# Forgetting attention: two heads side by side in the array, and later weight pieces

## The chip, the cores and the metric

The kernel runs on one core of a Trainium2 chip. The metric is the device time of one execution in microseconds, the median of the runs.

## What is computed

Two transformer blocks on 1024 rows of width 1024, in float32. The second block mixes three attentions: a latent one (4 heads, values of 128), a forgetting one (4 heads of 64) and a chunked one (4 heads of 64). The change is in the forgetting attention and in the latent one behind it. The forgetting attention, cut to what matters:

```python
def _fox(q, k, v, f_logit, f_bias):            # 4 heads of 64
    log_f = jax.nn.log_sigmoid(f_logit + f_bias)
    cum = jnp.cumsum(log_f, axis=1)
    def attend(args):                          # one block of 128 queries
        qb, cq, idx = args
        sc = jnp.einsum('bqhd,bkhd->bhqk', qb, k) * scale
        sc = sc + cq - cum_k                   # by head and position
        sc = jnp.where(k_pos <= q_pos, sc, -jnp.inf)
        p = jax.nn.softmax(sc, axis=-1)
        return jnp.einsum('bhqk,bkhd->bqhd', p, v)
```

The result is normalized by the root mean square of its rows (width 256), and together with the other two attentions it goes into the output projection `w_o`.

## The kernel before, in words

Each engine has a program of its own, written out by hand; engines wait for each other through counters (`wait_ge(signal, key)`). An engine's queue is strictly in order.

The attentions share the class `Heads`. There are 32 heads x = 4 i + h: block i of 128 queries (0 to 7), head h (0 to 3); in the forgetting attention (`Fox`) block i has i + 1 blocks of 128 keys. All engines run over the same steps `it`, which work on several heads at once:

- TensorE, step it: scores of head it (`L2994`, two products of the rounded and the remaining part of the keys, with a mask product for x < 16); transposes of the probabilities of head it - 2, in groups of up to four 128x128 blocks, into banks 4 and 5 (`L3008`); values of head it - 3 (`L3020`): for each block of keys a float32 matmul with the transposed probabilities `pt` as the loaded side and 64 columns of `fv` as the moving side, summed in bank 6 + i % 2. Then `later_pe`: a filler (in steps 0 to 8 a part of the missing query and key products), and in some steps the turn of finished rows.
- VectorE, step it: its share of the copies of the transposed probabilities (`copy_turned`, `L3052`), then the low half of the rows turned in the step before (`turned_dve`, `transposed_lo`, `L526`), mask (`L3687`) and negated maximum (`L3140`) of head it, and once per block the division by the sums (`L3112`) and the scaling of the normalized rows (`L3156`).
- ScalarE, step it: a filler copy, its share of the copies of the transposed probabilities (`L3054`; for x < 16 all of them), the exponentials of head it (`L3076`), once per block the squares (`L3092`), a weight piece if `sends` names one (`L456`), then the high half of the rows turned in this step (`later_act`, `transposed_hi`, `L518`).
- GpSimd: inverse roots (`L578`, `L571`) and the low halves of the weight pieces (`L462`).

Finished rows (256 wide) are turned by TensorE (`transposes`, `L508`) for the output projection: own block i at step 4 i + 9, the chunked attention's block i at step 4 i - 1. Each turn uses bank 6 + i % 2, i being the block turned. Bank use is guarded by `claim`: who takes a bank waits for the reader of what was in it last.

```python
def claim(b, sig, key):
    if b in held:
        PE.wait_ge(*held[b])
    held[b] = (sig, key)
```

After the last step come three query products of the latent attention (`before_last_turn`) and then the turn of the last block (`last_turn_pe`). Weights reach SBUF in pieces of 128x1024: SP loads a piece, ScalarE rounds it into `WH`, GpSimd takes the rest into `WL`, each a ring of five slots. Pieces 0 to 2 of `w_o` (`first["wo"]`) are sent at steps 5, 12 and 17 of the forgetting attention, pieces 3 and 4 at steps 13 and 16 of the latent one (`Latent`, the same steps with values of 128).

Of the kernel before, what the change touches and what calls it, by code (L numbers as in the profile page):

```python
# [238 lines left out]
def build(nc, ctx, I, out_dram):  # L239
# [2711 lines left out]
    class Heads:  # L2951
# [4 lines left out]
        n = 4 * NT  # L2956
        biased = False

# [17 lines left out]
        def mask_on_pe(self, x):  # L2976
            return False

        def pe(self):
            e = PE.e  # L2980
            freed = mx if self.biased else ex
            for it in range(self.n + 3):
                if it < self.n:
# [16 lines left out]
                if 2 <= it <= self.n + 1:  # L3000
                    x = it - 2
                    nb = self.view(x)[0] // 128
                    for g in range(0, nb, 4):
# [6 lines left out]
                        ins.then_inc(*tp.up((self.kind, x, g)))  # L3010
                if it >= 3:
                    x = it - 3
                    (i, h), nb = self.at(x), self.view(x)[0] // 128
                    b, k0 = 6 + i % 2, self.width(i)[0] // 128
                    if h == 0:
                        claim(b, ev, (self.kind, "o", i))
                    for g in range(0, nb, 4):
                        PE.wait_ge(ev if self.turns_by_dve(x, g) else cp, (self.kind, "pt", x, g))
                    for kb in range(nb):
                        ins = e.matmul(P[:, b, self.dv * h:self.dv * h + self.dv], self.pt(x, kb, 1)[:, 0, :],  # L3020
                                       self.v(h, k0 + kb), start=kb == 0, stop=kb == nb - 1)
                    ins.then_inc(*pv.up((self.kind, x)))
                self.later_pe(it)
            self.later_pe(self.n + 3)
            self.later_pe(self.n + 4)
            self.before_last_turn()
# [3 lines left out]
        def last_turn_pe(self):  # L3030
            self.later_pe(self.n + 5)
            PE.ends(self.kind)
# [7 lines left out]
        def copy_turned(self, port, x):  # L3040
            nb = self.view(x)[0] // 128
            for g in range(0, nb, 4):
# [3 lines left out]
                port.wait_ge(tp, (self.kind, x, g))  # L3046
                if x >= 2:
                    port.wait_ge(pv, (self.kind, x - 2))
# [10 lines left out]
        def act(self):  # L3059
            e = AC.e  # L3060
            self.began(AC)
            for it in range(self.n + 3):
                self.filling_act(it)
                if 2 <= it <= self.n + 1:
                    self.copy_turned(AC, it - 2)
                if it < self.n:
# [11 lines left out]
                if it >= 3 and self.at(it - 3)[1] == self.nh - 1:  # L3078
                    self.square(self.at(it - 3)[0])
# [3 lines left out]
            for it in range(self.n + 3, self.n + 6):  # L3083
                self.later_act(it)
# [10 lines left out]
        def dve(self):  # L3095
            e = DV.e
            self.began(DV)
            for it in range(self.n + 3):
# [5 lines left out]
                if it >= 3 and self.at(it - 3)[1] == self.nh - 1:  # L3104
                    i = self.at(it - 3)[0]
                    rsum, rden = head_rows(i)
                    DV.wait_ge(ex, (self.kind, it - 3))
                    e.reciprocal(rden, rsum).then_inc(*sm.up((self.kind, "rden", i)))
                    DV.wait_ge(sm, (self.kind, "rden", i))
                    DV.wait_ge(pv, (self.kind, it - 3))  # L3110
                    self.out_free(i)
                    e.tensor_tensor(self.outs[i % len(self.outs)][:, :].rearrange("p (h d) -> p h d", h=self.nh),  # L3112
                                    P[:, 6 + i % 2, 0:self.nh * self.dv].rearrange("p (h d) -> p h d", h=self.nh),
                                    rden.unsqueeze(2).to_broadcast([128, self.nh, self.dv]),
                                    ALU.mult).then_inc(*ev.up((self.kind, "o", i)))
                self.later_dve(it)
            for it in range(self.n + 3, self.n + 6):
                self.turned_dve(it - 1)
                self.later_dve(it)
            self.turned_dve(self.n + 5)  # L3120
            DV.ends(self.kind)
# [345 lines left out]
    def narrow_sp():  # L3467
# [12 lines left out]
        for th in range(2):  # L3480
            if th:
                load_to(first["wo"] + 2)
            SP.wait_ge(mm, ("fk", 1, th))
            for h in range(4):
                e.dma_start(fb[:, h, 512 * th:512 * th + 512],
                            f_dram[h, 512 * th:512 * th + 512].partition_broadcast(128)).then_inc(*l_fb.up((th, h)))
        load_to(first["wo"] + 4)

# [152 lines left out]
    class Fox(Heads):  # L3641
        kind, dv, biased = "fox", 64, True
        probs = [sb(f"p3_{i}", [128, 1024], off["ah"] + 4 * KB * i) for i in range(3)]
        turned = [[sb(f"pt3_0{i}", [128, 4, 128], off["ah"] + 12 * KB + 2 * KB * i) for i in range(2)],
                  [sb("pt3_10", [128, 4, 128], off["extra"] + 12 * KB), big("pt3_11", [128, 4, 128], 56)]]
        outs = [big(f"o3_{i}", [128, 256], 58 + i) for i in range(2)]
        squares = [big(f"sq3_{i}", [128, 256], 60 + i) for i in range(2)]
        sends = {1: first["uq"] + 1, 5: first["wo"], 12: first["wo"] + 1, 17: first["wo"] + 2}
        gain = (512, 768)
        k0 = 4  # L3650

        def pt(self, x, g, w):
            return self.turned[x % 2][g // 4][:, g % 4:g % 4 + w, :]

# [106 lines left out]

        def pool(self):
            for i in range(NT):
                for c in sorted(self.sends.values())[i:i + 1] if i < 3 else sorted(self.sends.values())[3:]:
                    low_to(c)
                self.roots(i)
# [124 lines left out]
    class Latent(Fox):  # L3891
        kind, dv, biased = "mla", 128, False
        maximum, turns_by_dve, before_last_turn = Heads.maximum, Heads.turns_by_dve, Heads.before_last_turn
# [52 lines left out]
        def pool(self):  # L3946
# [94 lines left out]
    class Cross(Fox):  # L4041
        kind, dv, biased = "cross", 128, False
        pairs = ((0,), (1,), (2,), (3,))
# [226 lines left out]
```

## Time and profile before

| | us |
|---|---|
| median of three runs | 2338.28 (2336.89 to 2339.26) |
| the profiled execution | 2338.47 |
| its span | 2336.70 |
| TensorE busy | 2301.3 |
| forgetting attention, first scores to first latent query product (1266.12 to 1356.92) | 90.80 |

The span is the time between the first and the last recorded instruction; 1.77 us lie around it. Times inside the trace count from the span's start. A busy matmul time is that of overlapping, pipelined instructions; how fast they follow each other is read from their starts.

### The profile page before, as it was taken

The numbers are of one execution on the slowest core, as the hardware profiler recorded it, in microseconds if no ns is written. First come the engines' busy times: TensorE is split into PE (matmuls) and PEld (weight loads), VectorE is DVE, ScalarE is ACT, GpSimd is POOL, SyncE is SP. The second block draws the span as 40 slices with busy tenths as digits, with TensorE's granted clock in tenths as the row PEclk, the third lists the DMA queues.
The fourth block names the chain that finished last, engine by engine and source line by source line (L and its number), as shares of the span: only waits on it lengthen the run. The fifth ranks groups of instructions, "written<-read, shape, count | busy, mean of one in ns | idle before, by whom it ended". The sixth has DMA issues, their size and how long they took to land. (4 is left out here: it accounts for less than half of the span.)

```text
span 2336.7 us, 30724 instructions
## 1 busy us (share of the span) xinstructions
PE 2301.3 (98%) x11602; PEld 1940.8 (83%) x11602; DVE 1427.9 (61%) x2219; ACT 967.9 (41%) x1966; POOL 867.3 (37%) x733
## 2 busy tenths in 40 slices
PE   9999999999999999999999999999999999999998
PEld 8787878888888888888998887888888888888887
DVE  7999924955454577775533767153594545457776
ACT  4126534533322345455635655134453233234443
POOL 2000125388787800032112121122338878770003
PEclk9999999999999999999999999999999999999999
DMA  5222124233233368664002100243223323336865
GB/s 158 52 63 74 54 91 132 85 117 117 86 117 104 117 241 282 213 214 125 19 19 71 46 5 19 64 155 125 88 67 117 118 86 117 104 119 245 283 214 198
DMA packets 219588, 275.84 MB, mean 118 GB/s; under 512 B 17259, under 2 KB 144972, under 8 KB 216626
## 3 DMA queue, kind: packets, MB, share of 16 engines
q1 hardware_dynamic: 200594, 210.31, 29.1%
q10 hardware_dynamic: 18848, 63.58, 6.9%
q8 instruction: 92, 1.51, 0.3%
q14 instruction: 54, 0.44, 0.1%
HBM read 205.27 MB, written 68.57 MB: 117 GB/s over the span
## 5 line engine op out<-in xcount | busy, mean ns | idle before, releaser
L496 PE MATMUL P<-ah,wh 128*128 128x512 f32 (+1 forms) x1136 | 441.2, 388 | 0.0
L498 PE MATMUL P<-ah,wl 128*128 128x512 f32 (+1 forms) x1136 | 438.8, 386 | 0.0
L497 PE MATMUL P<-al,wh 128*128 128x512 f32 (+1 forms) x1136 | 438.7, 386 | 0.0
L496 PE MATMUL P<-wh,ah 128*128 128x512 f32 (+2 forms) x1128 | 425.6, 377 | 0.0
L498 PE MATMUL P<-wh,al 128*128 128x512 f32 (+2 forms) x1128 | 423.3, 375 | 0.0
L497 PE MATMUL P<-wl,ah 128*128 128x512 f32 (+2 forms) x1128 | 422.9, 375 | 0.0
L578 POOL TENSOR_TENSOR stats<-stats,epsc 128x1 f32<-128x1 f32 x78 | 32.7, 419 | 771.2 <-ACT xn L1897 420.9
L498 PEld LDWEIGHTS P<-ah,wl 128*128 128x128 f32 x1136 | 213.3, 188 | 43.4
L496 PEld LDWEIGHTS P<-ah,wh 128*128 128x128 f32 x1136 | 213.4, 188 | 43.1 <-issue 0.4
L497 PEld LDWEIGHTS P<-al,wh 128*128 128x128 f32 x1136 | 213.4, 188 | 42.3
L498 PEld LDWEIGHTS P<-wh,al 128*128 128x128 f32 x1128 | 212.2, 188 | 36.7
L497 PEld LDWEIGHTS P<-wl,ah 128*128 128x128 f32 x1128 | 212.3, 188 | 36.4
L496 PEld LDWEIGHTS P<-wh,ah 128*128 128x128 f32 x1128 | 212.3, 188 | 36.3
L462 POOL TENSOR_TENSOR wl<-stage,wh 128x1024 fp32r<-128x1024 f32 (+3 forms) x43 | 99.4, 2316 | 302.4 <-ACT wh L456 302.0
L2850 POOL TENSOR_TENSOR wl<-ws,wh 128x512 fp32r<-128x512 f32 x154 | 204.1, 1347 | 3.0
L2850 POOL TENSOR_TENSOR wl<-stage,wh 128x512 fp32r<-128x512 f32 x128 | 181.7, 1436 | 49.9 <-DVE al L526 34.5
L2380 ACT ACTIVATE wh<-ws 128x512 fp32r<-128x512 f32 x160 | 96.5, 627 | 193.9 <-POOL ws L2843 189.5
L1190 DVE SCALAR_TENSOR_TENSOR acc<-hp,cwt,acc 128x1024 f32<-128x1024 f32 (+1 forms) x142 | 153.2, 1121 | 1.3
L2533 ACT ACTIVATE ah<-rf 128x512 fp32r<-128x512 f32 x154 | 95.6, 621 | 67.0 <-DMA rf<-ff_rows 63.7
L2741 DVE TENSOR_TENSOR al<-rf,ah 128x512 fp32r<-128x512 f32 x154 | 105.5, 685 | 20.9 <-ACT ah L2533 20.8
L456 ACT ACTIVATE wh<-stage 128x1024 fp32r<-128x1024 f32 (+2 forms) x68 | 68.8, 1014 | 78.1 <-PE P L498 49.6
L2380 ACT ACTIVATE wh<-stage 128x512 fp32r<-128x512 f32 x132 | 79.8, 621 | 45.2 <-PE P L498 30.1
(365 smaller groups left out, 4301.0 us busy)
## 6 DMA issues: line engine op xcount, KB each, us to landing
rf<-ff_rows SPq DMA_DIRECT2D x154, 256.0 KB, 5.2
stage<-in_w_down_dram SPq DMA_DIRECT2D x110, 256.0 KB, 3.8
ff_rows<-sb ACTq DMA_DIRECT2D x22, 1024.0 KB, 5.0
stage<-in_w_gu_dram SPq DMA_DIRECT2D x44, 512.0 KB, 5.2
stage<-in_w_in_dram SPq DMA_DIRECT2D x22, 512.0 KB, 3.9
stage<-in_w_gate_dram SPq DMA_DIRECT2D x22, 512.0 KB, 4.6
stage<-in_w_up_dram SPq DMA_DIRECT2D x22, 512.0 KB, 5.1
ff_rows<-uo ACTq DMA_DIRECT2D x22, 512.0 KB, 3.0
```

Of the source, the lines that this page charges most:

```text
L456: e.activation(WH[n % RING][:, 0:plan[n][0]], stage[place(n)][:, 0:plan[n][0]], ACT.Copy).then_inc(*wh.up(n))
L462: port.e.tensor_tensor(WL[n % RING][:, 0:w], stage[place(n)][:, 0:w], WH[n % RING][:, 0:w].bitcast(F32), ALU.subtract).then_inc(*sig.up(n))
L496: e.matmul(out, lh, rh, start=start, stop=False, skip_group_check=onto)
L497: e.matmul(out, lh, rl, start=False, stop=False, skip_group_check=onto)
L498: return e.matmul(out, ll, rh, start=False, stop=stop, skip_group_check=onto)
L578: PL.e.tensor_tensor(v, s, more, ALU.add).then_inc(*rs.up((key, "v")))
L1190: e.scalar_tensor_tensor(dst, src, cwt[:, c, w:w + 1], dst, ALU.mult, ALU.add).then_inc(*tap.up(key))
L2380: AC.e.activation(hi, src, ACT.Copy).then_inc(*wh.up((self.name, (m, op))))
L2533: AC.e.activation(self.rows_place(u)[0], RF[b][:, :], ACT.Copy).then_inc(*ah.up((self.name, "split", u)))
L2741: DV.e.tensor_tensor(lo, RF[self.row_buffer(u)[0]][:, :], hi.bitcast(F32), ALU.subtract).then_inc(*al.up((self.name, "split", u)))
L2850: PL.e.tensor_tensor(lo, src, hi.bitcast(F32), ALU.subtract).then_inc(*wl.up((self.name, (m, op))))
```

## The change

In the forgetting attention two heads (x - 1 and x, x odd) are summed together: the values are now the loaded side (64 columns), the transposed probabilities the moving side (128 columns), head x - 1 in partitions 0 to 63 and head x in 64 to 127 of bank 6. The sum is the transposed result, so ScalarE copies it to SBUF and TensorE turns it into bank 7, from where the division takes it. This happens every second step: values of (x - 1, x) at step x + 3, the turn at step x + 4, and the stage has one more step. The turns of finished rows all use bank 6, and the one of the last block now falls on a step ahead of the latent query products. A third pair of buffers for the transposed probabilities lies in slot 3 of `WH`; pieces 0 to 2 of `w_o` therefore are sent in the latent attention, at steps 14, 17 and 19, and pieces 3 and 4 at 21 and 23.

```diff
+        def steps(self):
+            return self.n + (4 if self.paired else 3)
+
+        def ended(self, it):
+
+            x = it - (4 if self.paired else 3)
+            return x // 4 if x >= 0 and x % 4 == 3 else None
+
+        def pair_values_pe(self, x):
+
+            (i, h), nb, k0 = self.at(x), self.view(x)[0] // 128, self.width(x // 4)[0] // 128
+            claim(6, cp, (self.kind, "pair", x))
+            for y in (x - 1, x):
+                for g in range(0, nb, 4):
+                    PE.wait_ge(ev if self.turns_by_dve(y, g) else cp, (self.kind, "pt", y, g))
+            for kb in range(nb):
+                for y in range(2):
+                    ins = PE.e.matmul(P[64 * y:64 * y + 64, 6, 0:128], self.v(h - 1 + y, k0 + kb),
+                                      self.pt(x - 1 + y, kb, 1)[:, 0, :], start=kb == 0, stop=kb == nb - 1)
+            ins.then_inc(*pv.up((self.kind, x)))
+
+        def pair_copy_act(self, x):
+            AC.wait_ge(pv, (self.kind, x))
+            if x >= 5:
+                AC.wait_ge(tp, (self.kind, "pair", x - 4))
+            AC.e.activation(self.pairs_out[x // 2 % 2][:, :], P[:, 6, 0:128], ACT.Copy).then_inc(
+                *cp.up((self.kind, "pair", x)))
+
+        def pair_turn_pe(self, x):
+            i, h = self.at(x)
+            if h == 1:
+                claim(7, ev, (self.kind, "o", i))
+            PE.wait_ge(cp, (self.kind, "pair", x))
+            PE.e.transpose(P[:, 7, 64 * h - 64:64 * h + 64], self.pairs_out[x // 2 % 2][:, :], ident[:, :]).then_inc(
+                *tp.up((self.kind, "pair", x)))
...
-            for it in range(self.n + 3):
+            for it in range(self.steps()):
...
-                if it >= 3:
+                if self.paired and it >= 5 and it % 2:
+                    self.pair_turn_pe(it - 4)
+                if self.paired and it >= 4 and it % 2 == 0 and it - 3 < self.n:
+                    self.pair_values_pe(it - 3)
+                if it >= 3 and not self.paired:
...
-            self.later_pe(self.n + 3)
-            self.later_pe(self.n + 4)
+            self.later_pe(self.steps())
+            self.later_pe(self.steps() + 1)
             self.before_last_turn()
...
-            self.later_pe(self.n + 5)
+            self.later_pe(self.steps() + 2)
...
-                if x >= 2:
+                if self.paired and x >= 3:
+                    port.wait_ge(pv, (self.kind, (x - 3) | 1))
+                elif x >= 2 and not self.paired:
                     port.wait_ge(pv, (self.kind, x - 2))
...
                 self.filling_act(it)
+                if self.paired and it >= 5 and it % 2:
+                    self.pair_copy_act(it - 4)
...
-                    DV.wait_ge(pv, (self.kind, it - 3))
+                    DV.wait_ge(*((tp, (self.kind, "pair", 4 * i + 3)) if self.paired else (pv, (self.kind, 4 * i + 3))))
...
             if th:
-                load_to(first["wo"] + 2)
+                load_to(first["wo"] + 1)
...
-        load_to(first["wo"] + 4)
...
     class Fox(Heads):
-        kind, dv, biased = "fox", 64, True
+        kind, dv, biased, paired = "fox", 64, True, True
...
+                  [sb(f"pt3_2{g}", [128, 4, 128], off["wh"] + (12 + 2 * g) * KB) for g in range(2)]]
+        pairs_out = [big(f"po3_{i}", [128, 128], 86.5 + i / 2) for i in range(2)]
...
-        sends = {1: first["uq"] + 1, 5: first["wo"], 12: first["wo"] + 1, 17: first["wo"] + 2}
+        sends = {1: first["uq"] + 1}
...
-            return self.turned[x % 2][g // 4][:, g % 4:g % 4 + w, :]
+            return self.turned[x % len(self.turned)][g // 4][:, g % 4:g % 4 + w, :]
...
-            if who is chunked:
-                return n, ("chunk", i), (6 + i % 2,)
-            return n, (self.kind, i), (6 + i % 2,)
+            return n, (who.kind, i), (6 if self.paired else 6 + i % 2,)
...
-            if it >= 7 and it % 4 == 3 and (it - 7) // 4 < NT:
-                i = (it - 7) // 4
+            i = (it - 8 if self.paired else it - 7) // 4
+            if it >= 7 and it % 4 == (0 if self.paired else 3) and i < NT:
...
     class Latent(Fox):
...
-        sends = {13: first["wo"] + 3, 16: first["wo"] + 4}
+        sends = {14: first["wo"], 17: first["wo"] + 1, 19: first["wo"] + 2, 21: first["wo"] + 3, 23: first["wo"] + 4}
...
             self.roots(2)
+            low_to(first["wo"] + 1)
+            self.roots(3)
             low_to(first["wo"] + 3)
-            self.roots(3)
+            self.roots(4)
             low_to(first["wo"] + 4)
-            for i in range(4, NT):
+            for i in range(5, NT):
```

## Rows read from the trace of the kernel before

**Rows 1.** The page, part 1: busy time, share of the span, instructions.

```profile
PE 2301.3 (98%) x11602; PEld 1940.8 (83%) x11602; DVE 1427.9 (61%) x2219; ACT 967.9 (41%) x1966; POOL 867.3 (37%) x733
```

**Rows 2.** Busy time by stretch: length, then engines, granted clock, DMA.

```profile
core 0: us, PE busy (x) PEld busy (x) DVE busy (x) ACT busy (x) POOL busy (x), PEclk, DMA share, GB/s
0.00:14.00 14.00, 9.30 (x43) 8.76 (x44) 4.35 (x8) 6.52 (x10) 3.69 (x9) 1.00 0.90 282
1266.12:1304.49 38.37, 36.28 (x223) 31.07 (x223) 22.05 (x57) 26.94 (x70) 8.09 (x7) 1.00 0.22 70
1304.49:1356.92 52.43, 52.13 (x427) 49.84 (x425) 37.20 (x89) 31.47 (x74) 6.08 (x11) 1.00 0.09 27
1356.92:1368.19 11.27, 11.27 (x52) 9.27 (x52) 6.68 (x12) 6.45 (x14) 3.72 (x4) 1.00 0.00 0
1368.19:1466.88 98.69, 95.26 (x606) 76.06 (x604) 69.24 (x133) 53.06 (x125) 17.74 (x22) 1.00 0.04 12
```

**Rows 3.** Instruction groups by form, 1266 to 1357: busy us, mean ns.

```profile
L3020 PE MATMUL P<-fv,pt 128*128 128x64 f32 x288 | 36.0, 270 | 1.9 <-ACT pt L3054 1.9
...
L3054 ACT ACTIVATE pt<-P 128x128 f32<-128x128 f32 x6 | 1.6, 267 | 1.5 <-PE P L3008 1.4
```

**Rows 4.** TensorE in order of time, steps 26 and 27: start, length.

```profile
1331.51 1.45 PE L3020 MATMUL P<-fv,pt 128*128 128x64 f32 x12
1332.77 1.07 PE L2994 MATMUL P<-fk,fqs 128*128 128x512 f32 x4
1333.67 0.93 PE L3008 MATMUL P<-ident,p 128*128 128x128 f32 x7
1334.44 1.67 PE L3020 MATMUL P<-fv,pt 128*128 128x64 f32 x14
```

**Rows 5.** TensorE in order of time, the latent attention's last values.

```profile
1465.17 1.95 PE L3020 MATMUL P<-mv,pt 128*128 128x128 f32 x16
```

**Rows 6.** Weight loads by form, whole span: busy us, mean ns.

```profile
L3020 PEld LDWEIGHTS P<-fv,pt 128*128 128x128 f32 x288 | 34.7, 192 | 2.7 <-issue 1.6 <-ACT pt L3054 1.1
...
L1103 PEld LDWEIGHTS P<-oh2a,rb2a 128*4 128x4 f32 x4 | 0.2, 84 | 1.5 <-issue 1.5
```

**Rows 7.** VectorE, then ScalarE, then VectorE in order of time, step 27.

```profile
1334.41 0.68 DVE L3052 COPY pt<-P 128x512 f32<-128x512 f32 x1
...
1335.33 1.09 DVE L3140 CUSTOM_DVE_ANT_0 p<-P,fb 128x896 f32<-128x896 f32 x1
...
1336.46 1.04 ACT L3076 ACTIVATE p<-p,stats 128x896 f32<-128x896 f32 x1 [0.58 <-DVE stats L3140]
...
1337.50 0.36 ACT L518 ACTIVATE ah<-P 128x256 fp32r<-128x256 f32 x1
...
1338.54 0.41 DVE L526 TENSOR_TENSOR al<-P,ah 128x256 fp32r<-128x256 f32 x1
```

**Rows 8.** Values' start and high half in steps 21 and 29.

```profile
1317.51 1.23 PE L3020 MATMUL P<-fv,pt 128*128 128x64 f32 x10
...
1320.81 0.36 ACT L518 ACTIVATE ah<-P 128x256 fp32r<-128x256 f32 x1
...
1341.13 1.67 PE L3020 MATMUL P<-fv,pt 128*128 128x64 f32 x14
...
1344.35 0.36 ACT L518 ACTIVATE ah<-P 128x256 fp32r<-128x256 f32 x1
```

**Rows 9.** The end of the stage: TensorE's first query product, VectorE's normalization.

```profile
1356.92 0.48 PE L496 MATMUL P<-ch,wh 128*128 128x512 f32 x1
...
1357.22 0.42 DVE L3112 TENSOR_TENSOR o<-P,stats 128x256 f32<-128x256 f32 x1 [0.88 <-PE P L3020]
...
1359.12 0.48 DVE L3156 SCALAR_TENSOR_TENSOR o<-o,stats,gout 128x256 f32<-128x256 f32 x1 [1.48 <-POOL stats L571]
```

**Rows 10.** A weight piece: ScalarE, GpSimd's low half, VectorE beside it.

```profile
1280.52 1.04 ACT L456 ACTIVATE wh<-stage 128x1024 fp32r<-128x1024 f32 x1
...
1284.81 2.41 POOL L462 TENSOR_TENSOR wl<-stage,wh 128x1024 fp32r<-128x1024 f32 x1
...
1284.88 2.62 DVE L3156 SCALAR_TENSOR_TENSOR o<-o,stats,gout 128x256 f32<-128x256 f32 x1
```

More of the change, by code:

```diff
@@ L2956, in build @@
         n = 4 * NT
-        biased = False
+        biased, paired = False, False
         def pt(self, x, g, w):
@@ L3061, in act @@
             self.began(AC)
-            for it in range(self.n + 3):
+            for it in range(self.steps()):
                 self.filling_act(it)
+                if self.paired and it >= 5 and it % 2:
+                    self.pair_copy_act(it - 4)
                 if 2 <= it <= self.n + 1:
@@ L3077, in act @@
                                  scale=-1.0 if self.biased else 1.0, accum_out=head_rows(i)[0][:, h:h + 1]).then_inc(*ex.up((self.kind, it)))
-                if it >= 3 and self.at(it - 3)[1] == self.nh - 1:
-                    self.square(self.at(it - 3)[0])
+                if self.ended(it) is not None:
+                    self.square(self.ended(it))
                 if it in self.sends:
@@ L3082, in act @@
                 self.later_act(it)
-            for it in range(self.n + 3, self.n + 6):
+            for it in range(self.steps(), self.steps() + 3):
                 self.later_act(it)
@@ L3097, in dve @@
             self.began(DV)
-            for it in range(self.n + 3):
+            for it in range(self.steps()):
                 if 2 <= it <= self.n + 1:
@@ L3103, in dve @@
                     self.maximum(it)
-                if it >= 3 and self.at(it - 3)[1] == self.nh - 1:
-                    i = self.at(it - 3)[0]
+                if self.ended(it) is not None:
+                    i = self.ended(it)
+                    b = 7 if self.paired else 6 + i % 2
                     rsum, rden = head_rows(i)
-                    DV.wait_ge(ex, (self.kind, it - 3))
+                    DV.wait_ge(ex, (self.kind, 4 * i + 3))
                     e.reciprocal(rden, rsum).then_inc(*sm.up((self.kind, "rden", i)))
                     DV.wait_ge(sm, (self.kind, "rden", i))
-                    DV.wait_ge(pv, (self.kind, it - 3))
+                    DV.wait_ge(*((tp, (self.kind, "pair", 4 * i + 3)) if self.paired else (pv, (self.kind, 4 * i + 3))))
                     self.out_free(i)
                     e.tensor_tensor(self.outs[i % len(self.outs)][:, :].rearrange("p (h d) -> p h d", h=self.nh),
-                                    P[:, 6 + i % 2, 0:self.nh * self.dv].rearrange("p (h d) -> p h d", h=self.nh),
+                                    P[:, b, 0:self.nh * self.dv].rearrange("p (h d) -> p h d", h=self.nh),
                                     rden.unsqueeze(2).to_broadcast([128, self.nh, self.dv]),
@@ L3116, in dve @@
                 self.later_dve(it)
-            for it in range(self.n + 3, self.n + 6):
+            for it in range(self.steps(), self.steps() + 3):
                 self.turned_dve(it - 1)
                 self.later_dve(it)
-            self.turned_dve(self.n + 5)
+            self.turned_dve(self.steps() + 2)
             DV.ends(self.kind)
@@ L3641, in build @@
     class Fox(Heads):
-        kind, dv, biased = "fox", 64, True
+        kind, dv, biased, paired = "fox", 64, True, True
         probs = [sb(f"p3_{i}", [128, 1024], off["ah"] + 4 * KB * i) for i in range(3)]
         turned = [[sb(f"pt3_0{i}", [128, 4, 128], off["ah"] + 12 * KB + 2 * KB * i) for i in range(2)],
-                  [sb("pt3_10", [128, 4, 128], off["extra"] + 12 * KB), big("pt3_11", [128, 4, 128], 56)]]
+                  [sb("pt3_10", [128, 4, 128], off["extra"] + 12 * KB), big("pt3_11", [128, 4, 128], 56)],
+                  [sb(f"pt3_2{g}", [128, 4, 128], off["wh"] + (12 + 2 * g) * KB) for g in range(2)]]
+        pairs_out = [big(f"po3_{i}", [128, 128], 86.5 + i / 2) for i in range(2)]
         outs = [big(f"o3_{i}", [128, 256], 58 + i) for i in range(2)]
         squares = [big(f"sq3_{i}", [128, 256], 60 + i) for i in range(2)]
-        sends = {1: first["uq"] + 1, 5: first["wo"], 12: first["wo"] + 1, 17: first["wo"] + 2}
+        sends = {1: first["uq"] + 1}
         gain = (512, 768)
@@ L3762, in pool @@
         def pool(self):
+            low_to(first["uq"] + 1)
             for i in range(NT):
-                for c in sorted(self.sends.values())[i:i + 1] if i < 3 else sorted(self.sends.values())[3:]:
-                    low_to(c)
                 self.roots(i)
@@ L3891, in build @@
     class Latent(Fox):
-        kind, dv, biased = "mla", 128, False
+        kind, dv, biased, paired = "mla", 128, False, False
         maximum, turns_by_dve, before_last_turn = Heads.maximum, Heads.turns_by_dve, Heads.before_last_turn
@@ L4041, in build @@
     class Cross(Fox):
-        kind, dv, biased = "cross", 128, False
+        kind, dv, biased, paired = "cross", 128, False, False
         pairs = ((0,), (1,), (2,), (3,))
```

## The prediction

> **What bounds the kernel now.** I read the page's busy times first, then the busy times by stretch, then the order in time of each engine inside the forgetting attention, last the waits. TensorE is busy for 98% of the span [rows 1]. In the attention itself (38.37 us until the scores of step 16, 52.43 us from there to the first query product of the latent attention) it is busy for 36.28 and 52.13 us, and in the 11.27 us after it for all of them [rows 2]. So whatever TensorE no longer does comes off the end, and whatever it is made to wait is added, since its queue is in order. The 288 value passes (144 blocks, each matmul recorded as two passes) are the largest group [rows 3]. A run of 14 passes lasts 1.67 us, 0.27 us of it the last one, so they follow each other every (1.67 - 0.27) / 13 = 0.108 us [rows 4, 3]; with the gaps around a run I take 0.11. The values cost 288 x 0.11 = 31.7 us.
>
> **The change, part by part.** E is an even step `it`, O an odd one.
>
> *The products.* A block of one head was 2 passes with 128 columns loaded and 64 moving. Now it is 2 passes with 64 loaded and 128 moving, the two heads in the two halves of the array. No row shows 64 columns loaded, nor two products side by side. The latent values move 128 columns at (1.95 - 0.27) / 15 = 0.112 us a pass [rows 5]: a wider moving side costs nothing. Lower bound: the halves run together, and a block of both heads costs 2 x 0.11 = 0.22 us. Upper bound: one after the other, 4 x 0.11 = 0.44, as before. Loads that do not hide behind products (recorded with 84 ns for 4 columns and 192 for 128, so some 0.13 for 64 [rows 6]) would go beyond; I keep that as a tail. I take the lower bound, since the products write different partitions and nothing in the trace ties one half to the other. The Trainium skill, TensorE: Matmul & The Clock Gate, Part 3, gives a gain of 2.38 for three column tiles, which as an estimate makes 0.28 us of a block pair; no run here shows it yet, and the sum by it would be 4 us more (68 block pairs x 0.06). Taken alone, 0.22 saves 72 x 2 x 0.11 = 15.8 us.
>
> *The extra turn.* 16 turns at 0.11 = 1.8 us on TensorE, and 16 copies of 128x128 on ScalarE, 0.27 us each like the small copies of `pt` [rows 3]; these hide in ScalarE's idle time (31.47 us busy of 52.43 [rows 2]).
>
> *The bank.* This part decides. Before, value sums and turns of finished rows (L508) alternate between banks 6 and 7, each in the one that the other isn't using. Now `turn_args` gives bank 6 to every turn, and every pair of heads is summed in bank 6 too. Each O from 7 to 29 ends with such a turn (3 and 33 too), and `claim` makes the values of the next E wait until VectorE has read it (L526). What lies between, in the order of the queues: TensorE ends the transposes of O; VectorE copies its group, masks, takes the maximum; ScalarE takes the exponentials, and only behind them the high half (L518); VectorE takes the low half. The rows show this walk for O = 27: transposes end (the values start) at 1334.44, copy 1334.41, maximum 1335.33, exponentials 1336.46, high half 1337.50 to 1337.86. That is 3.42 us, and with 0.42 + 0.05 for the low half 3.9 us [rows 4, 7]. O = 21 gives 1317.51 to 1321.17 = 3.66, O = 29 gives 1341.13 to 1344.71 = 3.58 [rows 8]; 23 and 25 between them, read the same way, 3.90 and 3.45. Before, nobody waited for it. Now TensorE has only the scores and transposes of E to fill it with, 0.90 + 0.77 us at 896 columns [rows 4]. It stands still some 2 us in each pair of steps. It doesn't catch up either: the walk begins behind the transposes of O, which are behind the last values on TensorE's own queue, so one turn of the loop takes values + scores(O) + transposes(O) + walk.
>
> The loop from the values of E to those of E + 2: the blocks at 0.22, scores about 0.1 more for each 128 columns and transposes 0.11 a block, both from the row at 896, the walk from the rows; 0.4 more of it at 19, 23, 27, where the squares (L3092) now come ahead of the high half (at 23 half of that is already in the row's 3.90, which has L3112 in it):
> 16: 0.87 + 0.72 + 0.46 + 2.9 = 4.95; 18: 0.87 + 0.72 + 0.55 + 4.0 = 6.15; 20: 1.1 + 0.78 + 0.55 + 4.1 = 6.5; 22: 1.1 + 0.78 + 0.66 + 4.4 = 6.9; 24: 1.3 + 0.9 + 0.66 + 3.9 = 6.8; 26: 1.3 + 0.9 + 0.77 + 4.3 = 7.3; 28: 1.5 + 1.0 + 0.77 + 4.05 = 7.3. In sum 45.9 us. The walks of 17 and 19 (2.9 and 4.0) are estimates, shorter for the smaller widths. The values of 16 start 2.5 us after its scores (the walk of 15, already under way).
>
> *The tail.* After the values of 30 (1.5) come scores and transposes of 31 (1.0 + 0.87), together 3.4. Then, in TensorE's order: a turn and transposes 0.1 + 0.87, values of 28 and 29 1.73, a wait of some 0.5 for the exponentials of 31, transposes 0.87, two turns 0.25, bank 6 again (copy, high half, low half) 1.7, the last values 1.73, ScalarE's copy and the turn 0.6. In the old order three query products of the latent attention stood ahead of the last rows' turn: they ran from 1356.92 while the normalization (L3112 at 1357.22, square, roots, L3156 until 1359.60) went on [rows 9]. Now the turn comes at step 37, ahead of them, and TensorE waits for that chain, 2.7 us. That is 11.0. From the scores of 16 to the query products: 2.5 + 45.9 + 3.4 + 11.0 = 62.8, against 52.4 [rows 2]: +10.4 us.
>
> *Steps 0 to 15.* Fillers keep TensorE busy to step 8. Four block pairs there cost 0.9 less than eight blocks did; the values of 4 and 8 wait some 0.5 each. From 9 on ScalarE and VectorE set the pace, and the waits for bank 6 at 10, 12 and 14 take what the shorter values give. I take +0.7, between -2 and +3.
>
> *Weight pieces.* Three copies of about 1 us on ScalarE and three lower halves of 2.4 us on GpSimd [rows 10] leave this stage and join two others in the latent attention, where ScalarE is busy 53.06 of 98.69 us and GpSimd 17.74 [rows 2]. What goes is the slow L3156 at step 7 (2.62 us beside a lower half, against 0.48 alone [rows 10, 9]), under fillers. SP asks for one piece fewer ahead of the second half of `fb`, so `fb` isn't later. The last piece is sent at step 23 of 32, well before the output projection begins at the end of that stretch; if ScalarE's idle time doesn't cover them, three pieces cost 3 us. I take +0.5, up to +3.
>
> **Sum.** 10.4 + 0.7 + 0.5 = +11.6 us. The profiled execution took 2338.47 us (the span's 2336.70 and 1.77 around it), 0.19 above the median of the runs. 2338.3 + 11.6 = 2349.9 us. A measurement tells a change from none beyond about 0.2%, 4.7 us.
>
> *Drains.* Behind the values of 26 the scores followed after 12 passes with no gap [rows 4]; there all was at full width. The Trainium skill, TensorEngine Tiling (Array Packing), Key Properties, states that changing the tiling mode drains the array. By that rule, as an estimate, each of 16 groups would expose 0.27 - 0.11 = 0.16 us, 2.6 us in all, and the time would be 2352.5. It speaks against the change; no row can show it.
>
> **Rivals.**
> A (52%): as above, halves together, bank 6 makes TensorE wait. 2349.9, own range 2345 to 2355.
> B (24%): the halves run one after the other. For it: four passes go through one queue, and no row has two at once. The values are in the loop, so each of 68 block pairs from step 10 on adds 0.22: +15, 2365.
> C (12%): the waits for bank 6 are half as long, because VectorE and ScalarE, idle 29% and 40% of that stretch [rows 2], do their part earlier than the old order shows. 12 waits x 0.9 us less = -11: 2339, no change to be seen.
> D (9%), the other side: the wait doesn't bind. -15.8 + 1.8 + 4 for the tail + 0.5 = -9.5: 2328.8. It decides from the point where the walk is shorter than scores and transposes of E (1.67 us at 896 columns); against it, the high half alone ends 3.42 us into the walk.
> E (3%): loads stand between the products, over 2370. TensorE's clock gets no term: at the start it was granted 1.00 (2.4 GHz) with 9.30 us busy in 14 [rows 2].
>
> The range takes in A, B and the upper part of C: 2340 to 2366. Faster 0.09 (D), within 0.2% 0.14 (C and the edge of A), slower 0.77.
>
> **What would show it.** Right: idle time of TensorE ahead of the values, ended by VectorE's L526, 15 to 20 us in some 12 waits of up to 2 us; one more of 2 to 3 us before the last L508; the stage from the first scores (1266.12) to the first query product 11 us longer. Products: four passes of a block pair start within 0.22 us (A) or 0.44 (B). Drains: a gap behind each group of values. Wrong: little waiting on L526 (C, D), or new idle time in the latent attention (weight pieces).

## The result, and the profile after

The changed kernel took 2355.5 us (median of 4 runs, 2352.2 to 2356.3) against 2338.8 us (4 runs, 2336.9 to 2339.4): a ratio of 1.0073 [1.0061, 1.0084], 16.7 us more. The forecast was 2349.9 us in a range from 2340 to 2366; rival A, the account that it rests on, gave itself 2345 to 2355, and the median lies just above that.

The profiled execution took 2356.3 us, its span 2354.5. The waits of TensorE between 1260 and 1400 us (engine and line waiting, engine and line waited for, us in all, times, longest):

```profile
PE P L2996 <- DVE al L526: 18.0, 14, 2.2
PE P L508 <- DVE o L3201: 2.5, 1, 2.5
PE P L3012 <- ACT po L3004: 1.8, 3, 1.0
```

L2996 is the paired values, L3012 the turn (transpose) of a pair's result, L508 here the turn of the last finished rows. The values wait for VectorE's low half of the turned rows, as forecast (15 to 20 us in some 12 waits of up to 2 us), and the last turn waits 2.5 us for the normalization (forecast 2.7). The stretches that answer to [rows 2], the last one longer, up to the latent attention's last turn (L508); columns as there:

```profile
1267.00:1306.54 39.54, 34.76 (x220) 28.01 (x221) 19.66 (x55) 26.61 (x74) 3.33 (x5) 1.00 0.16 56
1306.54:1373.82 67.28, 48.85 (x448) 41.63 (x446) 38.59 (x93) 33.68 (x84) 4.42 (x12) 0.94 0.02 5
1373.82:1387.46 13.64, 13.64 (x51) 11.02 (x50) 6.60 (x12) 6.46 (x12) 3.72 (x3) 0.79 0.00 0
1387.46:1489.65 102.19, 99.71 (x627) 80.08 (x626) 68.03 (x133) 56.43 (x130) 24.84 (x27) 1.00 0.08 27
```

Against before: steps 0 to 15 +1.17 us; from there to the first query product +14.85 (67.28 against 52.43, forecast +10.4); the query products' stretch +2.37 (13.64 against 11.27, forecast nothing); the latent attention -1.40 (102.19 against 103.59 for the same stretch before, forecast +0.5). The stage began 0.9 us later in this execution; in the other variants of the changed kernel below, whose code up to there is the same, it began between 1264.6 and 1265.8. So a microsecond ahead of the stage is scatter between executions. The granted clock is no longer 1.00: 0.94 and 0.79. TensorE in order of time, at several places of the stage after:

```profile
1308.98 1.09 PE L2996 MATMUL P<-pt,fv 128*64 128x128 f32 x16 [1.09 <-DVE al L526]
1310.00 0.90 PE L3030 MATMUL P<-fk,fqs 128*128 128x512 f32 x4
...
1320.17 1.31 PE L2996 MATMUL P<-pt,fv 128*64 128x128 f32 x20 [2.24 <-DVE al L526]
1321.41 1.65 PE L3030 MATMUL P<-fk,fqs 128*128 128x512 f32 x4
1322.86 1.27 PE L3044 MATMUL P<-ident,p 128*128 128x128 f32 x5
...
1328.93 0.97 PE L3030 MATMUL P<-fk,fqs 128*128 128x512 f32 x4
...
1334.50 2.30 PE L2996 MATMUL P<-pt,fv 128*64 128x128 f32 x24 [2.15 <-DVE al L526]
1336.73 1.86 PE L3030 MATMUL P<-fk,fqs 128*128 128x512 f32 x4
...
1350.46 1.75 PE L2996 MATMUL P<-pt,fv 128*64 128x128 f32 x28 [2.06 <-DVE al L526]
1352.14 1.19 PE L3030 MATMUL P<-fk,fqs 128*128 128x512 f32 x4
...
1368.26 1.97 PE L2996 MATMUL P<-pt,fv 128*64 128x128 f32 x32 [1.09 <-DVE al L526]
...
1373.48 0.69 PE L508 MATMUL P<-ident,o 128*128 128x128 f32 x2 [2.54 <-DVE o L3201]
1373.82 0.78 PE L496 MATMUL P<-ch,wh 128*128 128x512 f32 x1
1374.39 0.63 PE L497 MATMUL P<-cl,wh 128*128 128x512 f32 x1
1374.82 0.63 PE L498 MATMUL P<-ch,wl 128*128 128x512 f32 x1
```

Three things are to be read here.

**The halves do run together.** 32 passes, eight blocks of both heads, last 1.97 us: (1.97 - 0.27) / 31 = 0.055 us a pass, 0.22 for a block pair. Rival B, one half after the other, is out. The Trainium skill, TensorE: Matmul & The Clock Gate, Part 3, gives a gain of 2.38 for three column tiles, which as an estimate made 0.28; the trace gives 0.22.

**Behind a group of values there is a small gap.** 28 passes at 0.055 are 1.54 us, but the scores follow after 1.68 (1350.46 to 1352.14): 0.14 us more. 16 passes give 1.02 against 0.88, again 0.14. Before, 12 passes of 0.108 were followed after 1.26 [rows 4], without a gap. 16 groups make 2.2 us. The Trainium skill, TensorEngine Tiling (Array Packing), Key Properties, says that a change of the tiling mode drains the array; the page gives no duration, the estimate made for it was 0.16 a group, and the trace agrees in size. It can't tell a drain from the last pass's own half being busy for 0.055 us longer.

**Behind some waits everything takes nearly twice as long.** Four products of the scores took 1.65 us behind the wait of 2.24 (the same width took 0.97 at 1328.93), and behind the last wait of 2.54 the query products start 0.43 us apart instead of 0.23. The granted clock says why:

```profile
1321.41:1324.20 2.79, 2.79 (x13) 2.60 (x12) 0.56 (x2) 1.17 (x4) 0.00 (x0) 0.51 0.00 0
...
1373.48:1379.09 5.61, 5.61 (x15) 4.46 (x15) 0.42 (x1) 0.38 (x1) 0.00 (x0) 0.50 0.00 0
```

0.51 and 0.50 of 2.4 GHz is the lower level, 1.2 GHz. The prediction gave the clock no term. In this trace it fell behind waits of 2.24 and 2.15 us and around the one of 2.54; behind those of 2.06, 1.89, 1.79 and 1.73 the products ran at full speed.

### The profile page after: what moved, and what is told of

Its sections match the earlier page's. It is cut to its first block and busy times, and to the rows that moved or that the text cites. A ratio compares the mean times of both kernels' runs of the same rounds, so it can differ in the third digit from the quotient of the medians.

```text
span 2354.5 us, 30736 instructions
## 1 busy us (share of the span) xinstructions
PE 2298.6 (98%) x11618; PEld 1931.7 (82%) x11618; DVE 1423.7 (60%) x2219; ACT 972.4 (41%) x1982; POOL 866.7 (37%) x733
## 5 line engine op out<-in xcount | busy, mean ns | idle before, releaser
L456 ACT ACTIVATE wh<-stage 128x1024 fp32r<-128x1024 f32 (+2 forms) x68 | 68.8, 1015 | 78.1 <-PE P L498 48.6
```

What stands on the lines that cost most here:

```text
L456: e.activation(WH[n % RING][:, 0:plan[n][0]], stage[place(n)][:, 0:plan[n][0]], ACT.Copy).then_inc(*wh.up(n))
```

## The experiments

All are changes of the changed kernel, but for e5_weights. Each ratio is against runs of the kernel before on the same chip.

### Is it the order of the queues? Two moves

e1_hi: ScalarE takes the high half ahead of the exponentials, from step 9 on.

```diff
                     self.copy_turned(AC, it - 2)
+                if self.early(it):
+                    self.later_act(it)
                 if it < self.n:
...
-                self.later_act(it)
+                if not self.early(it):
+                    self.later_act(it)
```

> The changed kernel; from step 9 on ScalarE takes the high half of the turned rows (L518) before the exponentials of the step and no longer behind them. Theory (the wait for bank 6 is a walk through the queues, and the exponentials are part of it): the walk loses the exponentials, but VectorE still takes the low half only in the next step, behind its copy of the transposes of E. The waits of TensorE for L526 fall from 18.0 us to about 10, single ones from 2 to about 1.3, and the two stretches of half clock at steps 22 and 26 go with them (3.3 us): 2355.5 - 8 - 3 = 2344 to 2348. Rival (ScalarE and VectorE simply have too much to do for the shorter TensorE program, bank or no bank): the order within ScalarE's queue does nothing, 2353 to 2357.

Measured: 2344.6 us (7 runs, 2342.6 to 2346.8), ratio 1.0027 [1.0016, 1.0037]. The values' waits fell to 10.8 us in 11, and the two slow places of the loop are gone. Another appeared in step 12, behind a wait of 1.73 us that the changed kernel has too, there followed by full speed (values of 12 passes in 1.43 us instead of 0.88).

e2_hi_lo: the same, and VectorE takes the low half right behind its maximum.

```diff
                 if it < self.n:
                     self.maximum(it)
+                if self.early(it):
+                    self.low_dve(it)
...
         def turned_dve(self, it):
             self.filling_dve(it)
+            if not self.early(it):
+                self.low_dve(it)
+
+        def low_dve(self, it):
```

> As e1, and VectorE takes the low half (L526) in the same step, right behind its maximum. Theory: bank 6 is free some 0.3 us after TensorE gets there, the waits for L526 fall under 5 us in sum, and what is left of the change's gain shows up to the pace that VectorE and ScalarE set: 2355.5 - 13 - 3 = 2339 (2335 to 2344). Rival (their load is the bound): as in e1 no gain, 2353 to 2357, the idle time merely gets another releaser.

Measured: 2339.6 us (11 runs, 2338.8 to 2343.0), ratio 1.0007 [0.9999, 1.0016]. TensorE's waits:

```profile
PE P L3015 <- ACT po L3007: 5.7, 9, 1.8
PE P L508 <- DVE o L3211: 2.5, 1, 2.5
PE P L2999 <- DVE al L526: 1.9, 3, 1.1
```

The values' wait for bank 6 went from 18.0 to 1.9 us with the same bank and the same work, only in another order on two queues. 15.9 us of the 16.7 are gone with it, so the rival, which expected no gain, is out; TensorE now waits more for ScalarE's copy of the pair (L3007, 5.7 us). No product of the loop ran at half clock any more; the query products behind the 2.54 us wait still did, nine of them 0.43 us apart:

```profile
1357.67 0.44 PE L508 MATMUL P<-ident,o 128*128 128x128 f32 x2 [2.54 <-DVE o L3211]
1357.86 0.66 PE L496 MATMUL P<-ch,wh 128*128 128x512 f32 x1
1358.31 0.63 PE L497 MATMUL P<-cl,wh 128*128 128x512 f32 x1
1358.74 0.63 PE L498 MATMUL P<-ch,wl 128*128 128x512 f32 x1
```

### The last turn alone

e3_last: the last pair's step and its turn stay, but the turn of the last rows goes back behind the three query products.

```diff
-            self.later_pe(self.steps() + 1)
             self.before_last_turn()
+            self.later_pe(self.steps() + 1)
```

> The changed kernel; only the turn of the last rows is moved back behind the three latent query products. Theory (the stall of 2.54 us before that turn, and the half clock of the 13 products behind it, belong together): both go, 2.5 + 2.3 = 4.8 us, 2350.7, and the granted clock of the 11 to 14 us after the stage returns to 1.00. Rival (the clock fell because of the stalls of the stage as a whole): only the stall goes, 2353.0, and the products still start 0.43 us apart for some 5 us.

Measured: 2352.2 us (5 runs, 2349.1 to 2353.4), ratio 1.0058 [1.0045, 1.0071], 3.3 us under the changed kernel, between what the theory (2350.7) and its rival (2353.0) gave. The trace decides: the wait is gone, and the query products keep their pace from the first one on, 0.23 us apart:

```profile
1370.24 0.33 PE L3012 MATMUL P<-ident,po 128*128 128x128 f32 x1 [0.38 <-ACT po L3004]
1370.34 0.47 PE L496 MATMUL P<-ch,wh 128*128 128x512 f32 x1
1370.65 0.40 PE L497 MATMUL P<-cl,wh 128*128 128x512 f32 x1
1370.88 0.39 PE L498 MATMUL P<-ch,wl 128*128 128x512 f32 x1
```

From its first scores to those of the latent attention the stage took 115.81 us instead of 120.46, that is 4.65 less: 3.08 up to the first query product (the wait of 2.54, and the turn itself, which now stands behind the products), 2.42 in the query products (the clock), and 0.85 more in steps 0 to 15. There, at 1300.5, the clock fell behind a wait of 1.72 us that the changed kernel has as well, with the same code, and that is followed by full speed in its trace. 0.9 comes back in the latent attention (103.10 against 102.19), most of it in its second step, which needs 1.68 us instead of 0.92 when the turn is behind the products. The two slow places in the loop stayed.

### The clock alone

e7_fill: no wait is taken away, but two of them are filled in part with work that nobody needs.

```diff
+            if x in (17, 21):
+                it = x + 4
...
+                    for y, part in enumerate(keys):
+                        PE.e.matmul(P[:, p[w // size], 0:n], self.q(g, j), part, start=y == 0, stop=y == len(keys) - 1)
             claim(6, cp, (self.kind, "pair", x))
```

> Kernel: the change, and before two of its sixteen pair values (those of 20 and 24 block passes, at 1320.17 and 1334.50 us of its trace, behind waits of 2.24 and 2.15 us) TensorE computes the next step's scores once more than needed, into the bank that they get anyway; they are computed again in their own place. That is 0.9 us of work inside each wait; no wait is removed and nothing else moves. Theory (TensorE's clock falls to its lower level behind idle stretches that long, and the two stretches at half clock cost 1.6 and 1.7 us): with the idle time at 1.3 us the scores and turns behind both run at full length (0.88 and 0.63 us instead of 1.65 and 1.27), and the time is 2355.5 - 3.3 = 2352.2, ratio 1.0059. Rival (the slow stretches do not come from the idle time but from what the stage's mix of work draws): they stay where they are, or move a step on, and the time is 2355.5 or more.

Measured: 2352.8 us (5 runs, 2351.8 to 2356.1), ratio 1.0066 [1.0052, 1.0080], 2.7 us less for 8 products more. The changed kernel's own runs reach from 2352.2 to 2356.3, so the medians alone show no gain. Its TensorE (L2999 is the filling, L3006 the values, L3040 the scores, L3054 the transposes):

```profile
1316.88 0.96 PE L2999 MATMUL P<-fk,fqs 128*128 128x512 f32 x4 [0.16 <-DVE stats L3195]
1318.96 1.31 PE L3006 MATMUL P<-pt,fv 128*64 128x128 f32 x20 [1.12 <-DVE al L526]
1320.20 0.98 PE L3040 MATMUL P<-fk,fqs 128*128 128x512 f32 x4
...
1325.39 1.36 PE L3006 MATMUL P<-pt,fv 128*64 128x128 f32 x20 [1.98 <-DVE al L526]
1326.68 1.65 PE L3040 MATMUL P<-fk,fqs 128*128 128x512 f32 x4
1328.12 1.48 PE L3054 MATMUL P<-ident,p 128*128 128x128 f32 x6
...
1333.36 1.53 PE L3006 MATMUL P<-pt,fv 128*64 128x128 f32 x24 [0.89 <-DVE al L526]
1334.82 1.08 PE L3040 MATMUL P<-fk,fqs 128*128 128x512 f32 x4
```

Both filled waits are followed by products of full length: from the first filled group of values to the next 6.43 us instead of 7.51, from the second 7.00 instead of 8.57. Between them a slow stretch appeared behind an unfilled wait of 1.98 us, where 1.47 had stood before (7.97 against 6.82). That takes 1.15 of the 2.65 us back. A further slow stretch begins in step 12, ahead of both fillings, behind the wait of 1.73 us that the changed kernel passes at full speed; with it steps 0 to 15 last 0.82 us longer (40.36 against 39.54). The slow time in the query products was 1.1 us less. The whole stage is 1.85 us shorter (118.61 against 120.46), with three slow stretches in it as before.

What this shows is limited. With 1.12 and 0.89 us of idle time in place of 2.24 and 2.15, the products behind ran at full clock in both places, as the theory has it. The rival's "they move a step on" is true of one of the two, and a third fell where nothing had been touched. The full lengths at the widths concerned are 0.97 us for the scores and 0.74 for five transposes; the 0.88 and 0.63 of the expectation are those of a narrower block.

Taken over all ten traces, TensorE has 34 waits of 1.7 us or more between 1260 and 1400 us. 17 of them are followed by, or end in, a stretch at 1.2 GHz, and no stretch at 1.2 GHz in that time stands without one. The kernel before and e5_weights have no such wait (their longest is 1.2 us) and no slow stretch. But which of the waits it is isn't settled by their length: that of 1.72 or 1.73 us ahead of step 12's values was followed by full speed in the changed kernel and by half speed in e3_last and e7_fill, with the same code up to there. What decides stays open.

### The halves apart

e6_apart: in each pair all blocks of one head come first, then all of the other.

```diff
-            for kb in range(nb):
-                for y in range(2):
+            for y in range(2):
+                for kb in range(nb):
```

> The changed kernel with the two heads' products in another order: all blocks of the one head, then all of the other, in place of block by block in turns. If the measured 0.055 us a pass comes from the two halves of the array working at the same time, it needs neighbours in different halves: passes 0.11 us apart, and 60 to 68 block pairs in the loop at 0.22 more: +13 to +15, about 2369. Rival (a load of 64 columns is half as long, and that alone makes a pass half as long): no change, passes 0.055 us apart, 2355.

Measured: 2363.2 us (4 runs, 2361.9 to 2364.6), ratio 1.0106 [1.0090, 1.0121].

```profile
1371.51 3.33 PE L2996 MATMUL P<-pt,fv 128*64 128x128 f32 x32
```

(3.33 - 0.27) / 31 = 0.099 us a pass against 0.055: the same passes, nearly one after the other. The gain of the change's products needs neighbours in the queue that lie in different halves; the rival, that a load of 64 columns alone makes a pass half as long, is out. The price is smaller than the 13 to 15 us expected, since short groups lose less: from the groups' lengths at full clock (1.14 against 0.88, 1.58 against 1.09, 2.02 against 1.31, 2.45 against 1.53, 2.89 against 1.75, 3.33 against 1.97), two of each, it is 9.8 us.

The trace's stage, from its first scores to those of the latent attention, is 9.3 us longer (129.72 against 120.46). Besides the 9.8 it holds 2.6 less in the query products, which here ran at full clock behind the 2.54 us wait, and some 2 more ahead of them, where the clock fell in four places (behind 1.72, 2.25, 2.16 and 2.07 us) instead of two. The span grew by 7.6 only, because this execution came to the stage 1.7 us earlier.

### The weight pieces alone

e5_weights: the kernel before with the later pieces (`sends`, the places of `low_to` and `load_to`) and nothing else.

```diff
-        sends = {1: first["uq"] + 1, 5: first["wo"], 12: first["wo"] + 1, 17: first["wo"] + 2}
+        sends = {1: first["uq"] + 1}
...
-        sends = {13: first["wo"] + 3, 16: first["wo"] + 4}
+        sends = {14: first["wo"], 17: first["wo"] + 1, 19: first["wo"] + 2, 21: first["wo"] + 3, 23: first["wo"] + 4}
```

> Kernel: the kernel before, with only the other half of the change: the output weight's pieces are split and sent later, in the latent stage. Its pair values stay as they were. By the prediction's step this costs 0.5 us (2338.8 + 0.5 = 2339.3, ratio 1.0002). By the trace of the changed kernel, where the latent stage took 97.29 us instead of 98.69 and the stretch before the forgetting steps 1.2 + 0.9 us more, it gains 1.4 us there (2337.4, ratio 0.9994) unless the loss ahead of it belongs to the weights too, in which case it is 2338 to 2340.

Measured: 2334.8 us (11 runs, 2334.4 to 2337.0), ratio 0.9986 [0.9978, 0.9995]: 3.6 us faster than the kernel before. The expectation's largest gain was 1.4. Its stretches (to the scores of step 16, then to the first scores of the latent attention):

```profile
1265.00:1302.06 37.06, 35.78 (x223) 31.00 (x223) 19.86 (x57) 25.27 (x68) 3.33 (x5) 1.00 0.18 57
1302.06:1365.20 63.14, 63.14 (x478) 59.05 (x475) 43.98 (x101) 36.98 (x87) 7.42 (x14) 1.00 0.02 5
```

37.06 us instead of 38.37, 63.14 instead of 63.70, and 103.08 instead of 103.59 in the latent attention: -2.4 us. The remaining 1.1 us lies ahead of the first scores, where executions of the same code differ by more than that; the interval of the gain reaches from 1.2 to 5.1 us.

Where do the 1.31 us of the first stretch come from? The scaling that had taken 2.62 us beside a lower half on GpSimd [rows 10] takes 0.48 now, but TensorE had work all through it (5.00 of the 5.00 us from 1284 to 1289 before). 0.82 us of the 1.31 stand at one place, ahead of the values of step 14. First the kernel before, then e5_weights:

```profile
1300.23 1.04 ACT L456 ACTIVATE wh<-stage 128x1024 fp32r<-128x1024 f32 x1
1301.18 0.47 ACT L3054 ACTIVATE pt<-P 128x384 f32<-128x384 f32 x1
...
1300.38 0.66 PE L3008 MATMUL P<-ident,p 128*128 128x128 f32 x4
1301.70 0.88 PE L3020 MATMUL P<-fv,pt 128*128 128x64 f32 x6 [0.66 <-ACT pt L3054]
```

```profile
1298.75 0.47 ACT L3054 ACTIVATE pt<-P 128x384 f32<-128x384 f32 x1
...
1298.89 0.66 PE L3008 MATMUL P<-ident,p 128*128 128x128 f32 x4
1299.39 0.78 PE L3020 MATMUL P<-fv,pt 128*128 128x64 f32 x6
```

ScalarE rounded the piece sent at step 12 (L456, 1.04 us) ahead of the copy of the transposed probabilities for which TensorE waited. With the piece gone the copy comes in time, and the values follow the transposes after 0.50 us instead of 1.32.

### All moves together

e4_both is e2_hi_lo with the move of e3_last.

> Kernel: the change with three moves together: ScalarE takes the pair's high halves (L518) ahead of the exps of its step, VectorE takes L526 right behind its maximum, and the last turn stands behind three query products again. Theory (waits for the bank of the pair's values, and the clock that falls behind long waits): the run with the first two moves gave 2339.6; the third takes away the last wait of 2.5 us and the half clock behind it, in which about nine query products took 0.43 us instead of 0.23 (1.8 us). 2339.6 - 2.5 - 1.8 = 2335.3, ratio 0.9985; with the wait moved only and the clock kept, 2337.8. No stretch at half clock should be left between the first forgetting step and the latent stage. Rival (nothing gained: what is saved ahead of the query products comes back as a wait in the three steps behind them): 2339 to 2340.

Measured: 2337.1 us (11 runs, 2335.3 to 2338.9), ratio 0.9995 [0.9986, 1.0004]. 2.5 us under e2_hi_lo, not 4.3; the clock was 1.00 in both stretches of the stage. The 4.3 us are there up to the latent attention (the stage takes 101.17 us instead of 105.49), but 0.9 comes back in it, as in e3_last (103.10 against 102.16): the rival had that place right. The rest lies ahead of the stage, in the scatter. The stage against that of e5_weights shows what the pairing itself costs (same columns):

```profile
1265.63:1305.26 39.63, 34.90 (x220) 28.00 (x221) 19.65 (x55) 26.76 (x74) 3.34 (x5) 1.00 0.17 56
1305.26:1366.80 61.54, 57.50 (x496) 47.66 (x495) 43.90 (x103) 40.01 (x96) 7.42 (x14) 1.00 0.02 6
```

TensorE is busy 92.4 us instead of 98.9, but idle for 8.8 instead of 1.3. Pairing costs 2.6 us in steps 0 to 15, where ScalarE is busy 26.76 of 39.63 us and 3.8 of the 5.7 us of waits for its pair copy lie, and gains 1.6 behind them.

e8_late: e4_both with the turn of a pair behind the scores of the next step.

```diff
-                if self.paired and it >= 5 and it % 2:
-                    self.pair_turn_pe(it - 4)
...
                     ins.then_inc(*sc.up((self.kind, it)))
+                if self.paired and it >= 6 and it % 2 == 0:
+                    self.pair_turn_pe(it - 5)
```

> Kernel: the combination run before (high and low halves earlier, last turn back), with one more move: the turn of a pair's result stands behind the scores of the next step, not ahead of them, so that ScalarE's copy of the pair has one step's scores (0.9 us) more to be done. Theory (what is left of the change's cost are TensorE's waits for that copy, 5.7 us in nine of them, 3.8 us of it in the first sixteen steps, where three are long, 1.0, 1.0 and 1.8 us): about 0.8 us of each long wait goes and the short ones vanish, 2337.1 - 3 = 2334, ratio 0.998, about where the later weight pieces alone are (2334.8). Rival (a place moved is a wait moved: the normalization, and the values behind it, wait for the later turn instead): 2337 to 2339.

Measured: 2339.2 us (11 runs, 2337.3 to 2340.7), ratio 1.0003 [0.9994, 1.0012]; the rival was right:

```profile
PE P L508 <- ACT po L3007: 5.0, 8, 1.7
PE P L2999 <- DVE al L526: 3.6, 3, 2.1
```

Two things happened. The turn of finished rows (L508) claims bank 6, and so waits for the same copy of the pair that empties it: 5.4 us in all for that copy, against 5.7. And the normalization waits for the later turn, as the rival said. In step 8 VectorE stands still for 2.63 us ahead of the division, so its low half comes late, and TensorE's values wait 2.11 us for it where e4_both waits 0.25:

```profile
1286.73 0.42 DVE L3170 TENSOR_TENSOR o<-P,stats 128x256 f32<-128x256 f32 x1 [2.63 <-PE P L3015]
...
1288.47 0.42 DVE L526 TENSOR_TENSOR al<-P,ah 128x256 fp32r<-128x256 f32 x1
...
1288.95 1.12 PE L2999 MATMUL P<-pt,fv 128*64 128x128 f32 x8 [2.11 <-DVE al L526]
```

Behind that wait the clock fell once more, and steps 0 to 15 last 42.43 us instead of 39.63, 2.80 more. As long as values and turns share the bank, moving the pair's turn moves the wait and doesn't remove it.

## Why the prediction was right, and where its sum was short

The mechanism was as forecast: a gain in the products that the shared bank turns into waits of TensorE. e2_hi_lo shows it by giving 15.9 us back with no bank changed. The size was 11.6 us against 16.7 measured, and part of the closeness is luck: a term that was left out (the clock, 5.2 us) and one with the wrong sign (the weight pieces) pull opposite ways.

- **Products.** Right: 0.22 us a block pair, and e6_apart prices the other case. Its 2363.2 us lies near rival B's 2365 by chance: B added 15 us to 2349.9, while the products in that order added 7.8 to 2355.5.
- **The loop.** Between the starts of the values of steps 16, 18, ... 30 the trace has 4.86, 6.33, 7.51, 6.82, 8.57, 7.39 and 7.57 us; the forecast had 4.95, 6.15, 6.5, 6.9, 6.8, 7.3 and 7.3. Five of seven lie within 0.3. The two others, 1.0 and 1.8 too short, are those that began behind the waits of 2.24 and 2.15 us and ran in part at half clock. Sum 49.1 against 45.9. In the forecast's row 22 the walk of 4.4 is 0.2 less than its own rule gives (3.90 + 0.47 + 0.2).
- **The first values** came 2.44 us after the scores of 16, forecast 2.5. **The tail** took 15.8 us, forecast 3.4 + 11.0 = 14.4, with 2.54 of the 2.7 us of wait: 1.4 short. In the trace 0.56 of it lies at the turn and transposes of step 32 (1.53 us against 0.97, 0.24 of it a wait for a copy), and 0.34 is the last turn itself, which the sum left out. No experiment splits it.
- **TensorE's clock** is the step that failed: "TensorE's clock gets no term". It was read off the start of the span (9.30 us busy of 14, granted 1.00), where nothing showed what 2 us of standing still in the middle of the work does. In the profiled execution it cost 1.0 + 1.8 us in the loop and 2.4 in the query products, 5.2 us. In e7_fill the first two places run at full clock with their waits filled, in e3_last the third with its wait gone; both have a slow stretch elsewhere instead. So the missing term is a spread: up to 2.4 us behind each wait of some 2 us, in about half of the cases.
- **Weight pieces.** Wrong sign: +0.5 forecast, -2.4 us in the trace of e5_weights and -3.6 by the medians. The prediction counted the slow scaling (2.62 us) as hidden "under fillers", and TensorE was indeed busy beside it. What it gave no credit for is ScalarE's copy of the piece at step 12, which had stood ahead of the copy that TensorE waited for.
- **The latent attention** took 1.4 us less; 0.5 of it stands in e5_weights too, and 0.7 is the second step that is shorter when the last turn is done earlier (0.92 us here and in e2_hi_lo, 1.64 before and 1.68 in e3_last).
- **Steps 0 to 15**: +1.17, forecast +0.7; it is the sum of -1.3 from the weight pieces (37.06 in e5_weights against 38.37) and +2.5 from the pairing (39.54 against 37.06).
- **Drains.** The term was left out as the smaller likelihood; 0.14 us a group is there. The loop's sums hit all the same, so another term of it was some 0.1 us too large.
- **Rivals C and D.** The order of before that C doubted does hold in the changed kernel: the full waits are there. D's 2328.8 us, a kernel in which the bank doesn't bind, wasn't reached even with the waits for L526 nearly gone: ScalarE's copy of the pair came next, and 2337.1 was the best.

Added up against the profiled spans: 11.6 + 4.5 (loop, tail and first values) + 0.5 (steps 0 to 15) + 0.9 (later start) + 2.4 (query products) - 1.9 (latent attention) = 18.0, measured 17.8.

The paired values were not run without the later weight pieces; if the two parts add up, they cost 16.7 + 3.6 = 20.3 us alone. The best version here is the kernel before with the later weight pieces; the paired values in their best order came 2.3 us behind it by the medians, with ranges that overlap (2335.3 to 2338.9 against 2334.4 to 2337.0). Pairing from step 16 on alone, where it gained 1.6 us, wasn't tried.

## What to carry to other kernels

When a change makes work cheaper and puts two uses into one buffer, walk from the last reader of the buffer back through every queue; what stands ahead of it there (exponentials, copies) is the price, and reordering it may give back nearly all of it at no cost. A new wait of about 2 us on TensorE carries a risk on top: in these traces half of the waits of 1.72 to 2.54 us were followed by a stretch at half clock, which cost from 0.8 to 2.4 us. One trace with full speed behind a wait doesn't promise it for the next. Split a change of two parts before judging it: here one was worth 3.6 us and vanished behind the other.

## What the hardware showed that was not expected

- TensorE's granted clock fell to 1.2 GHz behind single waits of 1.72 to 2.54 us in the middle of dense work, for stretches of about 3 to 6 us. The length of the wait alone didn't decide: 2.06 us was followed by full speed, 1.98 in e7_fill by half, 2.54 in e6_apart by full speed, and one of 1.73, in the same code, by full speed in the changed kernel and by half in e7_fill.
- Two products of 64 columns in the two halves of the array overlap only if they alternate in the queue: 0.055 us a pass, against 0.099 in runs of one half, at 32 passes a group.
- A VectorE instruction of 0.48 us took 2.62 beside GpSimd's lower half of a weight piece (2.41 us). It cost TensorE nothing there; a ScalarE copy of 1.04 us that stood ahead of one TensorE waited for cost 0.8.
